# Moving k's products and the decay triangle one half ahead of the low parts of the delta output

## What is computed

```python
kb = k * beta[..., None]
A = jnp.einsum('bhnid,bhnjd->bhnij', kb, k) * decay * strict
T = lax.linalg.triangular_solve(eye + A, jnp.broadcast_to(eye, A.shape),
                                left_side=True, lower=True, unit_diagonal=True)
u = jnp.einsum('bhnij,bhnjd->bhnid', T, v * beta[..., None])
w = jnp.einsum('bhnij,bhnjd->bhnid', T, kb * jnp.exp(gc)[..., None])
...
o_a = rmsnorm(o_a, g_dn_out[i]).reshape(B, S, DN_WIDTH).astype(x.dtype) * jax.nn.silu(z_a)
y_a = o_a @ w_br_a[i]
```

## Time and profile before

| | us |
|---|---|
| median of 3 runs | 2503.09 (2503.02 to 2505.01) |
| profiled execution | 2502.11 |
| its span | 2500.3 |
| TensorE busy | 2441.2 |
| VectorE busy | 1612.6 |
| ScalarE busy | 1173.4 |
| GpSimd busy | 122.0 |

### The profile page before, as it was taken

The page is one execution under the profiler, slowest core; times in us unless marked ns, Lnnn a source line. Parts: engine busy times, 40 slices in busy tenths (PEclk is TensorE's granted clock), DMA queues, the critical chain, the costliest instruction groups (busy, mean ns, idle before and its releaser), DMA issues.

```text
span 2500.3 us, 34436 instructions
## 1 busy us (share of the span) xinstructions
PE 2441.2 (98%) x13555; PEld 2011.5 (80%) x13555; DVE 1612.6 (64%) x2154; ACT 1173.4 (47%) x1521; POOL 122.0 (5%) x224
## 2 busy tenths in 40 slices
PE   7999999999999999999999899999999999999997
PEld 6878878777878787878888688888888888888886
DVE  5799999778585767646556664656555544555554
ACT  5444444474454535344455564445444444443443
POOL 3000000010010102010000010000000000000000
PEclk9999999999999999999999999999999999999999
DMA  7566666455343435558656455646465666685563
GB/s 238 182 214 199 202 208 207 158 185 186 114 151 109 150 120 173 189 189 287 211 186 200 160 197 168 217 160 216 163 210 169 225 196 191 197 285 186 189 225 108
DMA packets 226923, 470.10 MB, mean 188 GB/s; under 512 B 12217, under 2 KB 13090, under 8 KB 225634
## 3 DMA queue, kind: packets, MB, share of 16 engines
q1 hardware_dynamic: 214018, 418.57, 51.3%
q0 software_dynamic: 12768, 49.59, 5.6%
HBM read 445.05 MB, written 23.07 MB: 187 GB/s over the span
## 4 chain that ended last, share of the span: by engine, by line
PE 58%; DVE 1%; ACT 1%; issue 0%; POOL 0%; DVEq 0%; ACTq 0%; POOLq 0%
PE acc L2209 53%; PE aux L2239 1%; PE aux L2369 1%; PE aux L2657 0%; PE aux L2656 0%; DVE w_lo L1412 0%; PE aux L2225 0%; ACT w_hi L799 0%; PE aux L2663 0%; DVE cy L1686 0%; PE aux L2671 0%; PE aux L2672 0%; PE aux L2670 0%; PE aux L2648 0%; PE aux L2634 0%
## 5 line engine op out<-in xcount | busy, mean ns | idle before, releaser
L1412 DVE TENSOR_TENSOR w_lo<-raw,w_hi 128x1024 fp32r<-128x1024 f32 x790 | 965.2, 1224 | 812.2 <-ACT w_hi L799 800.8
L799 ACT CAST w_hi<-raw 128x1024 fp32r<-128x1024 f32 x790 | 827.0, 1049 | 1167.8 <-PE acc L2209 1158.1
L2209 PE MATMUL acc<-w_hi,r1h 128*128 128x512 f32 (+1 forms) x1920 | 762.9, 397 | 8.9 <-DVE w_lo L1412 4.8
L2209 PE MATMUL acc<-w_hi,r1l 128*128 128x512 f32 (+1 forms) x1920 | 746.0, 389 | 0.0
L2209 PE MATMUL acc<-w_lo,r1h 128*128 128x512 f32 (+1 forms) x1920 | 745.9, 389 | 0.0
L2209 PE MATMUL acc<-w_hi,r2h 128*128 128x512 f32 x1216 | 477.2, 392 | 2.4 <-DVE w_lo L1412 1.9
L2209 PE MATMUL acc<-w_hi,r2l 128*128 128x512 f32 x1216 | 473.5, 389 | 0.0
L2209 PE MATMUL acc<-w_lo,r2h 128*128 128x512 f32 x1216 | 473.3, 389 | 0.0
L2209 PEld LDWEIGHTS acc<-w_hi,r1h 128*128 128x128 f32 x1920 | 361.4, 188 | 91.6 <-DVE w_lo L1412 6.9
L2209 PEld LDWEIGHTS acc<-w_hi,r1l 128*128 128x128 f32 x1920 | 361.1, 188 | 75.7
L2209 PEld LDWEIGHTS acc<-w_lo,r1h 128*128 128x128 f32 x1920 | 361.7, 188 | 70.0 <-issue 1.0
(11 more groups left out here) (460 smaller groups left out, 1469.9 us busy)
## 6 DMA issues: line engine op xcount, KB each, us to landing
raw<-in_w_in SPq DMA_DIRECT2D x264, 1024.0 KB, 5.0
raw<-in_w_out SPq DMA_DIRECT2D x32, 1024.0 KB, 5.1
raw<-in_w_br_b SPq DMA_DIRECT2D x16, 1024.0 KB, 5.2
raw<-in_w_br_a SPq DMA_DIRECT2D x16, 1024.0 KB, 6.3
raw<-in_w_ple_gate SPq DMA_DIRECT2D x16, 1024.0 KB, 5.2
raw<-in_w_o_mla SPq DMA_DIRECT2D x16, 1024.0 KB, 5.2
raw<-in_w_o_conv SPq DMA_DIRECT2D x16, 1024.0 KB, 5.0
raw<-in_w_q_b SPq DMA_DIRECT2D x8, 1024.0 KB, 5.2
```

The source lines that it names most:

```text
L799: nc.scalar.copy(w_hi[:, h % HL, 0:n], raw[:, k % RAW, x * HALF:x * HALF + n]).then_inc(hi_ready, 1)
L1412: V.tensor_tensor(w_lo[:, h % HL, 0:n], raw[:, k % RAW, x * HALF:x * HALF + n], w_hi[:, h % HL, 0:n].bitcast(F32), ALU.subtract).then_inc( ...
L2209: ins = T.matmul(acc[:, s, x, 0:n], a[:, kt0 + k, xs_], w[:, h % HL, at], start=start and k == 0 and m == 0, stop=stop and k == kts - 1 an ...
```

## The change

On VectorE, `own` does the two products of k one half earlier (`hl == 30`) and the decay triangle right behind them instead of at `hl == 0` of the next pass. They now stand ahead of a w_lo split and of the two ol instructions. Since ktok no longer comes behind ol, TensorE waits for `oT_hi` and `oT_lo` itself before it overwrites the banks; in pass 1, where no delta output exists yet (`dv(2, 0)` is 0), these waits are left out.

```diff
@@ VectorE, own @@
-                if hl == 31:
+                if hl == 30:
                     dve.wait_ge(sem("cols_ready"), i + 1)
                     sig(V.tensor_tensor(th(ktok), th(ktok), over(col(2), DK), ALU.mult), "ktok_ready", i + 1)
                     sig(V.tensor_tensor(th(kb), th(ktok), over(col(3), DK), ALU.mult), "kb_ready", i + 1)
+                    sig(V.tensor_tensor(th(gm), rep(tri_c[:], TC2), over(col(7), SEQ_CHUNK), ALU.mult), "gm_ready", i + 1)
@@ VectorE, delta @@
-                if hl == 0:
-                    sig(V.tensor_tensor(th(gm), rep(tri_c[:], TC2), over(col(7), SEQ_CHUNK), ALU.mult), "gm_ready", dv(1, 1))
@@ TensorE, delta @@
                 if hl == 0:
+                    if dv(2, 0):
+                        pe.wait_ge(sem("oT_hi"), dv(2, 0))
+                        pe.wait_ge(sem("oT_lo"), dv(2, 0))
                     pe.wait_ge(sem("ktok_ready"), dv(1, 1))
                     per_head_tr(0, ktok, "kT_tr")
```

## The result

The changed kernel took 2508.72 us (median of 9 runs, 2506.70 to 2513.53), the one before 2503.02 in the same comparison (2502.02 to 2505.68). The ratio is 1.0024, its 95% interval 1.0014 to 1.0034: slower by 5.7 us. I had forecast 2505.2, with a range up to 2508.5. The profiled execution took 2508.72 us with a span of 2506.9, so 6.6 us more than the profiled one of before.

A forecast was written before the change was run, and what follows sets the result against it. TensorE, busy 2441.2 of 2500.3 us, was taken to bound the kernel. Its terms, +0.43 at the second and third change of block and +1.28 at the fourth, made +2.1: 2505.2 us, 8-in-10 range 2502.5 to 2508.5.

The forecast's parts named there:

- ol ends late: Last three changes of block: ol ends 3.33 us later, TensorE starts ktok's transposes 1.97 us later, waiting about 2.8 us.
- the waits for gm and bf: TensorE's waits in delta vanish: gm 0.54 at second and third change of block, 0.24 at fourth; bf 0.55 at second and third.
- the three changes of block: Second, third and fourth change of block, where TensorE newly waits for ol: +0.43, +0.43 and +1.28 us; the first costs 0.
- the sum: Late start less returned waits over the last three changes of block: +2.1 us, with no loss of clock.
- the covers: Slack costed at nothing: 9 us for GpSimd's columns, 6 us for w_lo of half 2, over 13 us for the last reload.
- the last of the unknown costs: TensorE's clock after the 2.8 us waits: no loss taken; other end 1.75 us at each of three places, +5.2.
- rival A: New waits at three changes of block cost TensorE its clock, some 3.5 us at 1.2 GHz each: 2510.4 us; chance 0.07.
- The sign that the prediction names for A: In the profile after, a granted clock under 1.00 around 730 us, the second change of block.
- B of the prediction: Waits for gm and bf stay because TensorE's lateness passes to VectorE through kbT: 2507.7 us; chance 0.07.
- C: VectorE makes up ol's 3.3 us; waits for kb, gm and bf go, 3.8 us saved: 2499.3 us; chance 0.04.
- D: All waits go, also 0.85 us ahead of ktok's transposes at three places; 6.4 us saved: 2496.7 us; chance 0.02.

The follow-up runs named there:

- e8: Changed kernel with TensorE's wait for ol filled by doing kb's transposes three times more: 2504.86 us, ratio 1.0010.
- e6: Kernel before, with only the decay triangle moved from half 0 of the next pass to right behind kb: 2502.02 us, ratio 0.9996.
- e10: The changed kernel run again with no edit: 2508.95 us, ratio 1.0021.
- e1: Changed kernel with the decay triangle put back at half 0, ktok and kb still one half ahead: 2507.10 us, ratio 1.0017.
- e2: Changed kernel with TensorE transposing kb before it waits for the low parts: 2506.74 us, ratio 1.0013.
- e9: Changed kernel with the product kb done twice on VectorE, so ol comes later and TensorE waits longer: 2516.45 us, ratio 1.0059.
- e4: Changed kernel with five extra float32 triangle products on TensorE ahead of its wait for ol: 2510.21 us.
- e5: Changed kernel with two extra float32 triangle products on TensorE ahead of its wait for ol: 2506.05 us, ratio 1.0016.
- e3: Changed kernel with ol also moved to half 30, ahead of ktok, kb and gm: 2501.98 us, ratio 0.9997.

## Why the prediction was wrong

**What was right.** Everything that could be counted. ol ends late by the three products ahead of it: TensorE's wait became 2.88 us, forecast 2.8. Half 1 to half 2 takes 735.26 - 731.98 = 3.28 us, forecast 3.28, and half 2 to half 4 takes 8.85, forecast 8.85, so the waits for gm and bf went. Without the clock's share the three changes of block cost, in e8, 0.55, 0.54 (880.64 - 863.53 = 17.11 against 16.57) and 1.39 us (half 0 to half 4: 1016.88 - 999.77 = 17.11 against 1014.48 - 998.76 = 15.72), where the sum has 0.43, 0.43 and 1.28: 2.5 us for 2.1. The median of e8, 2504.86, is the 2505.2 of the forecast within its spread. In the changed kernel's profile no reload, and at the changes of block no w_lo and no column of GpSimd, was waited for: the covers held.

**The step that failed** is the last of the unknown costs: "A wait of 2.8 lies between, 0.9 from the one and 2.3 from the other; I take no loss", and with it the chance of 0.07 for rival A. The loss taken at nothing is about 3.8 us of the 5.7 measured; the waits themselves make up the rest. I read one row, a wait of 1.91 us with full speed behind it, as a property of the length. It was one draw. The same wait at 538 us stands in all 13 profiles (1.89 to 1.93 us), and half speed follows it in 7 of them. A second wait of 1.93 us, for a w_lo split near 1440 us, stands in all 13 too; half speed follows that one in 2, e6 and e10. Over all profiles of this case half speed followed in

| wait | where | half speed after it |
|---|---|---|
| 0.85 us | three places; before, e6 | 0 of 6 |
| 1.45 to 1.57 us | near 1320 and 1490 us, all profiles | 0 of 26 |
| 1.89 to 1.93 us | at 538 us, all profiles | 7 of 13 |
| 1.93 us | near 1440 us, all profiles | 2 of 13 |
| 2.0 to 2.2 us | three places; e1, e2 | 3 of 6 |
| 2.9 us | three places; changed, e10 | 4 of 6 |
| 4.1 us | three places; e9 | 3 of 3 |
| 5.0 to 5.1 us | at 569 us, all profiles | 13 of 13 |
| filled to 0.8 us or less | three places; e4, e5, e8 | 0 of 9 |

What the fall looks like behind the wait near 1440 us, in e10:

```profile
1444.77 0.47 PE L2208 MATMUL acc<-w_hi,r2h 128*128 128x512 f32 x1 [1.93 <-DVE w_lo L1412]
...
1445.69 0.63 PE L2208 MATMUL acc<-w_hi,r2h 128*128 128x512 f32 x1
```

The counts are small: they show that the shortest waits never and the longest always were followed by half speed, but not how 1.9, 2.1 and 2.9 us rank among themselves. Length is also not all, since two waits of the same 1.9 us differ, 7 of 13 and 2 of 13.

So rival A was what happened, though not in each place in each execution. Its price was sized at 1.75 us for a place, half of one stretch of 3.5 us; the first profile gives 3.35 - 0.52 = 2.8 for the third change and 3.02 - 1.39 = 1.6 for the fourth. The third change's stretch is twice as long (granted clock 0.51 from 865.6 to 872.5 us), and the trace of before already had one of that length: after a wait of 7.32 us the granted clock is 0.51 from 1412 to 1419 us. The prediction's sentence that the trace shows 2.4 GHz everywhere but at 569 us overlooks it. Averaged over runs the clock's share is 2508.7 - 2504.9 = 3.8 us, about two places of three. The rival's 2508.7 for two places is where the measurement fell, but that is in part luck: it adds 2.1 us for the waits and 3.5 for the clock, while the waits alone cost 2.5 in e8, the two slow places of the first profile cost 4.5, and how many places are slow differs from profile to profile. The sign that the prediction names for A, a granted clock under 1.00 around 730 us, was not there in the first profile either; the fall stood at the other two places.

The Trainium skill ("TensorE: Matmul & The Clock Gate", Part 1) calls the count of slow matmuls at a kernel's start, before the clock rises, run-variable. No run here was made to show that for the rise; of the fall the traces show the like: after the same wait at 538 us TensorE kept full speed in 6 profiles and lost it in 7.

**Rivals.** B of the prediction (nothing comes back, 2507.7) has nearly the measured time and the wrong reason: both waits went. C and D were priced as if each wait were worth its length. e3 shows what D would have been: the waits for ktok and gm gone and about 1 us gained, not 6.4, since waits for kbT and bf took their place. The prediction had used that very stretch of VectorE to argue that bf would not come later; it should have used it to argue that nothing ahead of bf could gain.

**Open.** What in TensorE's past decides at which of two equal waits the clock falls is not settled by these runs. It need not be chance: the wait at 538 us ended between 537.41 and 538.88 us of the span, the five profiles in which it ended before 538.0 all kept full speed, and of the eight in which it ended at 538.19 or later seven lost it. So the moment at which the wait falls may count beside its length; no run moved a wait of one length in time to test it. e5 and e8 filled the wait with different kinds of work and differ by 1.2 us in their medians, with overlapping spreads (2504.55 to 2509.64 and 2503.24 to 2507.71); whether that is the 0.8 us of idle time left in e5 I did not try.

## What to carry to other kernels

Price a new wait on the busiest engine twice: its length less what it lets later waits save, and the stretch at half clock that may follow. One trace's row in which a wait of some length was followed by full speed is one draw; take a chance for it, not a verdict. And before counting a removed wait as a gain, find the next operand that the waiting engine needs from the same busy engine: at the second and third change of block less work ahead of that operand (0.93 us of copies) moved the end by 0.94 us, another order of it by 0.24.

## What the runs showed of the hardware that was not expected

- Half speed (1.2 GHz) followed a wait of 1.9 us in 9 of 26 cases, 7 of 13 at one place of the program and 2 of 13 at another; it never followed waits of 0.85 us (6 cases) or 1.45 to 1.57 us (26 cases), and always one of 5.0 us (13 cases).
- Filling the idle time with transposes whose result is thrown away kept full speed at all three places and made the kernel 3.9 us faster (2504.86 for 2508.72); two or five float32 products kept it too.
- The mean granted clock of a run follows its time: 0.991 in the slowest run of the changed kernel (2513.53) and 0.994 in the fastest (2506.70). The spread from run to run is no safe sign of a fall at the three places: 6.8 us over 9 and 4.0 over 11 runs of the changed kernel and 2.1 over 7 runs with five products, but 5.1 over 11 runs with two products, whose profile has full speed at all three.
